# Residual additions over four tiles, and the squares of two norms summed with one column of ones

## The chip, the cores and the metric

One core of a Trainium2 chip runs the whole program. The metric is the time of one execution in microseconds of device time; the kernel before was run three times. TensorE (PE in the profile) multiplies, VectorE (DVE) and ScalarE (ACT) work element by element, GpSimd (POOL) and SyncE (SP) mostly issue transfers here.

## What is computed

Two transformer-like blocks one behind the other on 256 tokens of width 2048. The place of the change is the residual path with its norms: the end of the first block, and the start of the second.

```python
def rms_norm(v, g):
    vf = v.astype(F32)
    y = vf * lax.rsqrt(jnp.mean(vf * vf, axis=-1, keepdims=True) + RMS_EPS)
    return (y * g.astype(F32)).astype(v.dtype)

# first block
y, yc = hybrid_mixer(h, hc, rows, not last, w_in[i], conv_p, ssd_p, fourier_out[i], rwkv_p, w_o[i])
x = x + g1 * rms_norm(y, norm_g[i, 1])
h = rms_norm(x, norm_g[i, 2]) * (1 + sc2) + sh2
x = x + g2 * rms_norm(sq_relu_mlp(h, mlp_up[i], mlp_down[i]), norm_g[i, 3])
# second block
h = rmsnorm(x, g_mix[l]) * (1.0 + sc1) + sh1
x = x + gt1 * hybrid_mixer_2(h, w_in[l], ...)
h = rmsnorm(x, g_ffn[l]) * (1.0 + sc2) + sh2
x = x + gt2 * conv_glu_ffn(h, w_ffn_gate[l], ...)
return rmsnorm(x, final_g)
```

## The kernel before

Everything is float32 and lies transposed: a tile is 128 of the 2048 features on the partitions by 256 tokens (`T`), and there are 16 tiles (`KT`). `xT` holds the residual, `hT` the normed input of the next products, `work` scratch, `ps` the eight PSUM banks. Weights stream in units of one megabyte (`ring`), and each is split into a rounded part (`round_unit`, L2662, ScalarE) and its remainder (`rest_unit`, L2667, VectorE), so that products of rounded halves give float32 accuracy (L2700 to L2704 and, for the first two units behind a norm, L2721 to L2725 in `twin_products`). The order of work on each engine is the order in which the code of the stages is written for it: for the part that matters, `Mix` (out-projection, norm of y, residual, norm of x), `Mlp`, `In2`, `Ffn2`. Engines wait for one another by counting semaphores.

A norm is an object of `Rms`. There are two sorts.
- The norms of y (`rms_y1` behind the out-projection, `rms_y2` behind the MLP) and two later ones of x (`rms_x3`, `rms_x4`) are *summed*: ScalarE squares each tile as it comes out of the products (`square_out`, L2556), VectorE adds the squares of all tiles but the last (`add_square`, L2565), and TensorE sums over the partitions with the squares as the stationary operand and one column of ones, once for each half of the tokens (L2582, and L2585 for the last tile). That leaves 128x2 numbers with the tokens on the partitions. ScalarE takes the root (L2605), VectorE the reciprocal (L2610), and TensorE spreads the two columns over all partitions (`spread_root`, L2594) into a PSUM bank, `rows`.
- The norms in front of the MLP and of the in-projection (`rms_x1`, `rms_x2`) are not: ScalarE squares pairs of tiles of `xT` into `hT` as the residual is added (L2602, `nadd` counts tiles added), TensorE sums them with a full 128x128 of ones as the stationary operand and each tile of squares as 256 moving columns (L2577), which leaves the sum on every partition at once. Root and reciprocal are then taken over 128x256 in `rtn` in SBUF.

`add_scaled` (L2624) adds a normed y to the residual: for each tile one multiplication by the spread root (L2628), and one tile later a multiply by the gain and add (L2632). `scale_split` (L2635) and `shift_round` (L2648) then scale, shift and split x for the products: L2640 and L2644 on VectorE, L2651 on ScalarE. In `Mix`, VectorE has one `rest_unit` between `add_scaled` and the norm of x. In `Mlp` the last steps are `rms_y2`, `add_scaled`, and `In2` begins with `rms_x2`.

Other lines named below: L409 turns modulation rows with two moving columns and 128x128 stationary, early in the kernel; L3561 multiplies a tile of `xT` by the final gain on ScalarE; L3687 multiplies groups of four tiles by the spread root at the very end; L2745 copies the first half of a unit's result out of PSUM.

Of the kernel before, what the change touches and what calls it, by code (L numbers as in the profile page):

```python
# [13 lines left out]
P = 128  # L14
D = 2048
# [160 lines left out]
def branch_kernel(nc, x_t, ctx_t, vecs, consts, smalls, smalls2, c_rows, mod_u, mod_r, ada_r, conv_u, ssd_u, rw_u, gate_u, bo_u, wo_u,  # L176
                  mlp_u, in2_u, out2_u, ffn_u, down2_u, out_t):
    ctx = ExitStack()
    with ctx:
# [2354 lines left out]
        class Rms:  # L2534


            def __init__(self, src, ready, summed=0, reset=1, last=None, turns=1):
# [11 lines left out]
                self.rows = rtn  # L2549
                if summed:  # L2550
                    self.spread = aux()
                    self.rows = ps[:, self.spread[0], 0:T]
# [18 lines left out]
            def tensor(self, pe):  # L2571
                acquire(pe, self.use)
                if not self.summed:
                    for kt in range(KT):
                        if kt % self.step == 0:
                            pe.wait_ge(nsq, self.first + kt // self.step + 1)
                        mm = pe.matmul(ps[:, self.use[0], 0:T], kc("ones"), self.squares[:, kt, :], start=kt == 0, stop=kt == KT - 1)  # L2577
                    mm.then_inc(bk.full[self.use[0]], 1)
                    return
                pe.wait_ge(sq_added, self.total)  # L2580
                for a in range(TT):
                    pe.matmul(ps[:, self.use[0], a:a + 1], sq_sum[:, a * P:(a + 1) * P], kc("ones", 0, 1), start=a == 0, stop=False)  # L2582
                pe.wait_ge(nsq, self.first + self.summed)
                for a in range(TT):
                    mm = pe.matmul(ps[:, self.use[0], a:a + 1], self.last[:, a * P:(a + 1) * P], kc("ones", 0, 1), start=False, stop=a == TT - 1)  # L2585
# [11 lines left out]
            def scalar(self, act):  # L2597
# [6 lines left out]
                to, n = (root[:, 0:TT], TT) if self.summed else (rtn, T)  # L2604
                emptied(self.use, act.activation(to, ps[:, self.use[0], 0:n], ACT.Sqrt, bias=eps(EPS_RMS), scale=1.0 / D))  # L2605

            def vector(self, dve):
                evacuated(dve, self.use)
                to = root[:, 0:TT] if self.summed else rtn
                dve.reciprocal(to, to).then_inc(nrs, 1)  # L2610
                if self.summed:
                    full(dve, self.spread)
                else:
                    dve.wait_ge(nrs, self.k)

            def read(self, eng):
                if self.summed:
                    eng.sem_inc(bk.free[self.spread[0]], 1)
# [5 lines left out]
        def add_scaled(dve, own, src, col, rms):  # L2624

            for kt in range(KT + 1):
                if kt < KT:
# [1270 lines left out]
```

## Time and profile before

| | us |
|---|---|
| median of 3 runs (lowest, highest) | 3307.74 (3307.04, 3309.56) |
| profiled execution, its own time | 3307.34 |
| its span | 3305.7 |
| PE busy | 3227.1 (98%) |
| DVE busy | 2204.6 (67%) |
| ACT busy | 1241.4 (38%) |

The span is the time from the first to the last instruction of the profiled execution. The busy times say how full each engine is, but not what sets the end; that is to be read from the chain of work that ended last and from the timeline around the two places where the changed lines run, about 1456 to 1475 us and 2198 to 2216 us. The granted clock is given as a share of 2.4 GHz: 1.00 is 2.4, 0.50 is 1.2.

### The profile page before, as it was taken

Reading aid. Unit: us, or ns where it says so; the run is one execution under the profiler, and the core shown is the slowest. Engines: PE = TensorE matmul, PEld = TensorE weight load, DVE = VectorE, ACT = ScalarE, POOL = GpSimd, SP = SyncE. Lnnn points to the kernel's source line nnn. Section 1 sums busy time; section 2 is a strip of 40 time slices with the busy share of each in tenths; the row PEclk is TensorE's granted clock in tenths of the full one; section 3 lists DMA queues with packets and bytes.
Section 4 is the critical chain, followed back from the end, with each engine's and each line's share of the span. In section 5 each row is a group of like instructions: output and inputs, shape, how many; then the busy total and the mean of one; then the engine's idle time right before and its main releaser. Section 6 shows DMA issues by size and latency. Waiting matters only on the chain.

```text
span 3305.7 us, 58756 instructions
## 1 busy us (share of the span) xinstructions
PE 3227.1 (98%) x23408; PEld 2700.4 (82%) x23408; DVE 2204.6 (67%) x3396; ACT 1241.4 (38%) x1686; POOL 196.2 (6%) x298
## 2 busy tenths in 40 slices
PE   7999999999999999989999999989999999999998
PEld 4764685478888999978888888878888888888887
DVE  2377656665655677667878777787666667667667
ACT  2202130144444421344344444444544443443444
POOL 0000000012122000000000000000000000000000
PEclk9999999999999999999999999999999999999999
DMA  9956727622222688637767777745445557656654
GB/s 408 364 204 229 277 86 258 241 84 89 89 92 98 234 353 349 228 140 258 276 244 271 256 256 259 255 169 180 161 153 178 191 190 261 210 190 241 225 179 156
DMA packets 101013, 709.02 MB, mean 214 GB/s; under 512 B 11200, under 2 KB 11328, under 8 KB 19520
## 3 DMA queue, kind: packets, MB, share of 16 engines
q1 hardware_dynamic: 73872, 525.89, 43.9%
q0 software_dynamic: 23184, 169.88, 13.9%
q10 hardware_dynamic: 3744, 10.23, 0.8%
q8 instruction: 155, 2.54, 0.3%
q14 instruction: 58, 0.48, 0.0%
HBM read 698.36 MB, written 7.60 MB: 214 GB/s over the span
## 4 chain that ended last, share of the span: by engine, by line
PE 92%; DVE 4%; DMA 2%; issue 1%; ACT 1%; DVEq 0%; SPq 0%; ACTq 0%; POOLq 0%
PE ps L2704 33%; PE ps L2703 17%; PE ps L632 11%; PE ps L2407 3%; PE ps L1099 3%; PE ps L399 2%; PE ps L2700 2%; PE ps L1819 2%; PE ps L1100 2%; PE ps L1101 2%; PE ps L1833 1%; PE ps L2389 1%; PE ps L2388 1%; PE ps L2390 1%; PE ps L1091 1%; PE ps L2701 1%
## 5 line engine op out<-in xcount | busy, mean ns | idle before, releaser
L2704 PE MATMUL ps<-hT_parts,rows_parts 128*128 128x512 f32 x3210 | 1130.6, 394 | 0.0
L2703 PE MATMUL ps<-hT_parts,ring_parts 128*128 128x256 f32 x3210 | 901.9, 281 | 1.7 <-DVE hT_parts L2676 1.6
L2667 DVE TENSOR_TENSOR ring_parts<-ring,rows_parts 128x2048 fp32r<-128x2048 f32 (+1 forms) x337 | 762.1, 2262 | 102.7 <-ACT rows_parts L2662 101.7
L2662 ACT ACTIVATE rows_parts<-ring 128x2048 fp32r<-128x2048 f32 (+1 forms) x337 | 639.4, 1897 | 406.2 <-DMA ring<-in_mlp_u 209.1
L2704 PEld LDWEIGHTS ps<-hT_parts,rows_parts 128*128 128x128 f32 x3210 | 604.2, 188 | 125.0
L2703 PEld LDWEIGHTS ps<-hT_parts,ring_parts 128*128 128x128 f32 x3210 | 607.9, 189 | 12.6 <-DVE hT_parts L2676 2.9
L2704 PE MATMUL ps<-work_parts,rows_parts 128*128 128x512 f32 x1616 | 570.1, 395 | 0.0
L2703 PE MATMUL ps<-work_parts,ring_parts 128*128 128x256 f32 x1616 | 454.2, 281 | 0.0
L632 PE MATMUL ps<-hT,ring 128*128 128x512 f32 (+1 forms) x1088 | 372.4, 505 | 0.0
L2704 PEld LDWEIGHTS ps<-work_parts,rows_parts 128*128 128x128 f32 x1616 | 304.2, 188 | 63.2
L632 PEld LDWEIGHTS ps<-hT,ring 128*128 128x128 f32 x1088 | 206.9, 190 | 163.4 <-issue 152.0
L2745 ACT ACTIVATE work<-ps 128x256 f32<-128x256 f32 (+1 forms) x220 | 84.3, 383 | 616.5 <-PE ps L2704 608.3
L2703 PEld LDWEIGHTS ps<-work_parts,ring_parts 128*128 128x128 f32 x1616 | 306.2, 189 | 5.1
L2750 DVE TENSOR_TENSOR work<-work,ps 128x256 f32<-128x256 f32 (+1 forms) x220 | 92.6, 421 | 258.0 <-ACT work L2745 245.7
L433 DVE CUSTOM_DVE_ANT_0 rows<-rows 128x2048 f32<-128x2048 f32 x64 | 146.5, 2288 | 33.4 <-DMA rows<-in_mod_r 33.4
L2515 DVE CUSTOM_DVE_ANT_0 work<-work,K 128x2048 f32<-128x2048 f32 x64 | 146.3, 2286 | 0.0
L2407 PE MATMUL ps<-work 128*128 128x256 f32 x576 | 125.6, 379 | 0.0
L2407 PEld LDWEIGHTS ps<-work 128*128 128x128 f32 x576 | 109.0, 190 | 14.3
L2135 DVE TENSOR_TENSOR work<-work,ps 128x64 f32<-128x64 f32 x288 | 42.8, 216 | 115.5 <-PE ps L1833 114.4
L433 DVE CUSTOM_DVE_ANT_0 rows<-rows,K 128x2048 f32<-128x2048 f32 x32 | 73.3, 2290 | 49.1 <-DMA rows<-in_ada_r 49.1
L2508 POOL DMA_DIRECT2D work<-in_ada_r x64 | 33.8, 528 | 1204.4 <-DVE g_acc L2515 1171.3
L2836 DVE TENSOR_TENSOR work<-work,ps 128x256 f32<-128x256 f32 (+1 forms) x112 | 46.9, 418 | 80.6 <-PE ps L2704 80.3
(495 smaller groups left out, 4532.5 us busy)
## 6 DMA issues: line engine op xcount, KB each, us to landing
ring<-in_mlp_u SPq DMA_DIRECT2D x128, 1024.0 KB, 5.0
ring<-in_ffn_u SPq DMA_DIRECT2D x88, 1024.0 KB, 4.8
rows<-in_mod_r POOLq DMA_DIRECT2D x64, 1024.0 KB, 5.2
ring<-in_gate_u SPq DMA_DIRECT2D x64, 1024.0 KB, 5.2
work<-in_ada_r POOLq DMA_DIRECT2D x64, 1024.0 KB, 5.2
ring<-in_in_u SPq DMA_DIRECT2D x36, 1024.0 KB, 4.8
rows<-in_ada_r POOLq DMA_DIRECT2D x32, 1024.0 KB, 9.0
ring<-in_down_u SPq DMA_DIRECT2D x32, 1024.0 KB, 4.9
```

What stands on the lines that cost most here:

```text
L399: mm = pe.matmul(ps[:, use[0], o % 2 * T:(o % 2 + 1) * T], wtile(u, 4 * o + k), hT[:, 4 * kq + k, 0:T], start=kq + k + o % 2 == 0, stop=kq ...
L433: dve.tensor_tensor_reduce(rows_buf[:, j, :], rows_buf[:, j, :], conditioning, 1.0, 0.0, ALU.mult, ALU.add, g_acc[:, j:j + 1]).then_inc(ro ...
L632: mm = pe.matmul(outs[o], wtile(u + o, kt), rhs(kt), start=kt == 0, stop=kt == KT - 1)
L1099: pe.matmul(out, high, kept_high(kt), start=kt == 0, stop=False)
L2407: mm = pe.matmul(ps[:, 3 + b, o * T:(o + 1) * T], bo_buf[:, at + kt, o * P:(o + 1) * P], src[:, kt, :], start=kt == 0, stop=kt == kts - 1)
L2515: dve.tensor_tensor_reduce(late_row, late_row, c2_row, 1.0, 0.0, ALU.mult, ALU.add, acc).then_inc(late_free, 1)
L2662: act.activation(unit_high(u)[:, 0:size], slot(u)[:, 0:size], ACT.Copy).then_inc(hi_done, 1)
L2667: dve.tensor_tensor(ring_parts[:, ring_slot(u), 0:size], slot(u)[:, 0:size], unit_high(u)[:, 0:size].bitcast(F32), ALU.subtract)\
L2703: pe.matmul(ps[:, b, low_half], low, top(kt), start=False, stop=False)
L2704: mm = pe.matmul(ps[:, b, :], high, both(kt), start=False, stop=kt == kts - 1)
L2745: act.activation(dst, ps[:, b:b + 1, half], ACT.Copy).then_inc(half_out, 1)
L2750: dve.tensor_tensor(dst, dst, ps[:, b:b + 1, half], ALU.add).then_inc(bk.free[b], 1)
```

## The change

`add_scaled` goes over four tiles at a time. The multiplication by the spread root is one instruction over 128x1024, with the row repeated, and the addition one over 128x1024 (for the last group two over 128x512). The gain is no longer part of the addition: ScalarE multiplies y by it beforehand with a scaled copy in place (`scale_tile`), counted in `merge_sum`. In the out-projection this follows each tile's square; behind the MLP two tiles are scaled ahead of the root and fourteen behind it.

The norms `rms_x1` and `rms_x2` sum their squares in the form of the summed norms: for each of the 16 tiles two products, squares stationary, one column of ones moving. Their root and reciprocal go over 128x2, and TensorE spreads the result into the bank of the norm of y before them (`bank`). The squaring on ScalarE stays as it is.

```diff
-                self.rows = rtn
-                if summed:
-                    self.spread = aux()
-                    self.rows = ps[:, self.spread[0], 0:T]
+                self.spread = bk.take(bank) if bank else aux()
+                self.rows = ps[:, self.spread[0], 0:T]
...
-                        mm = pe.matmul(ps[:, self.use[0], 0:T], kc("ones"), self.squares[:, kt, :], start=kt == 0, stop=kt == KT - 1)
-                    mm.then_inc(bk.full[self.use[0]], 1)
-                    return
+                        for a in range(TT):
+                            mm = pe.matmul(ps[:, self.use[0], a:a + 1], self.squares[:, kt, a * P:(a + 1) * P], kc("ones", 0, 1),
+                                           start=kt == 0 and a == 0, stop=kt == KT - 1 and a == TT - 1)
                 mm.then_inc(bk.full[self.use[0]], 1)
                 acquire(pe, self.spread)
                 pe.wait_ge(nrs, self.k)
...
-                to, n = (root[:, 0:TT], TT) if self.summed else (rtn, T)
-                emptied(self.use, act.activation(to, ps[:, self.use[0], 0:n], ACT.Sqrt, bias=eps(EPS_RMS), scale=1.0 / D))
+                emptied(self.use, act.activation(root[:, 0:TT], ps[:, self.use[0], 0:TT], ACT.Sqrt, bias=eps(EPS_RMS), scale=1.0 / D))
...
-                to = root[:, 0:TT] if self.summed else rtn
-                dve.reciprocal(to, to).then_inc(nrs, 1)
-                if self.summed:
-                    full(dve, self.spread)
-                else:
-                    dve.wait_ge(nrs, self.k)
+                dve.reciprocal(root[:, 0:TT], root[:, 0:TT]).then_inc(nrs, 1)
+                full(dve, self.spread)
...
-        def add_scaled(dve, own, src, col, rms):
-
-            for kt in range(KT + 1):
-                if kt < KT:
-                    own.step(dve.tensor_tensor(src[:, kt, :], src[:, kt, :], rms.rows, ALU.mult))
-                if kt:
-                    own.settle(1 if kt < KT else 0)
-                    t = kt - 1
-                    dve.scalar_tensor_tensor(xT[:, t, :], src[:, t, :], col[:, t:t + 1], xT[:, t, :], ALU.mult, ALU.add).then_inc(nadd, 1)
+        def scale_tile(act, y, gain):
+
+            act.activation(y, y, ACT.Copy, scale=gain).then_inc(merge_sum, 1)
+
+        def add_scaled(dve, own, src, rms, scaled):
+
+            for g in range(KT // 4 + 1):
+                if g < KT // 4:
+                    group = src[:, 4 * g:4 * g + 4, :]
+                    dve.wait_ge(merge_sum, scaled + 4 * (g + 1))
+                    own.step(dve.tensor_tensor(group, group, bc(rms.rows, 4), ALU.mult))
+                if g:
+                    own.settle(1 if g < KT // 4 else 0)
+                    size = 4 if g < KT // 4 else 2
+                    for t in range(4 * (g - 1), 4 * g, size):
+                        dve.tensor_tensor(xT[:, t:t + size, :], xT[:, t:t + size, :], src[:, t:t + size, :], ALU.add).then_inc(nadd, size)
             rms.read(dve)
...
-        rms_x1 = Rms(xT[:, :, :], lambda e, n: e.wait_ge(nadd, 2 * n + 2))
+        rms_x1 = Rms(xT[:, :, :], lambda e, n: e.wait_ge(nadd, 2 * n + 2), bank=rms_y1.spread[0])
...
-                        rms_y1.square_out(act, yT1[:, bass.ds(it * 4 + j, 1), :], sq1[:, bass.ds(it * 4 + j, 1), :])
+                        t = bass.ds(it * 4 + j, 1)
+                        rms_y1.square_out(act, yT1[:, t, :], sq1[:, t, :])
+                        scale_tile(act, yT1[:, t, :], gn1[:, t])
...
-                add_scaled(dve, own, yT1, gn1, rms_y1)
+                add_scaled(dve, own, yT1, rms_y1, 2 * PAIRS2)
...
+                for t in range(2):
+                    scale_tile(act, yT2[:, t, :], gn3[:, t:t + 1])
                 rms_y2.scalar(act)
+                for t in range(2, KT):
+                    scale_tile(act, yT2[:, t, :], gn3[:, t:t + 1])
...
-                add_scaled(dve, own, yT2, gn3, rms_y2)
+                add_scaled(dve, own, yT2, rms_y2, 2 * PAIRS2 + KT)
...
-        rms_x2 = Rms(xT[:, :, :], lambda e, n: e.wait_ge(nadd, KT + 2 * n + 2))
+        rms_x2 = Rms(xT[:, :, :], lambda e, n: e.wait_ge(nadd, KT + 2 * n + 2), bank=rms_y2.spread[0])
```

## Rows read from the trace of the kernel before

**Rows 1.** The page, chain of work that ended last, by engine

```profile
PE 92%; DVE 4%; DMA 2%; issue 1%; ACT 1%; DVEq 0%; SPq 0%; ACTq 0%; POOLq 0%
```

**Rows 2.** Timeline, VectorE: start us, us, engine, line, operation, count [idle before <-releaser]

```profile
1456.68 0.75 DVE L2628 TENSOR_TENSOR work<-work,ps 128x256 f32<-128x256 f32 x2 [0.87 <-PE ps L2594]
1457.35 0.48 DVE L2632 SCALAR_TENSOR_TENSOR xT<-work,coef,xT 128x256 f32<-128x256 f32 x1
...
1467.51 0.89 DVE L2632 SCALAR_TENSOR_TENSOR xT<-work,coef,xT 128x256 f32<-128x256 f32 x2
...
1472.58 1.28 DVE L2640 SCALAR_TENSOR_TENSOR hT<-xT,coef,work 128x256 f32<-128x256 f32 x3
```

**Rows 3.** Timeline, the same stretch, ScalarE

```profile
1458.59 0.63 ACT L2602 ACTIVATE hT<-xT 128x512 f32<-128x512 f32 x1 [1.18 <-DVE xT L2632]
...
1470.29 0.47 ACT L2605 ACTIVATE work<-ps,K 128x256 f32<-128x256 f32 x1 [1.22 <-PE ps L2577]
...
1487.11 0.38 ACT L2745 ACTIVATE work<-ps 128x256 f32<-128x256 f32 x1 [2.41 <-PE ps L2725]
```

**Rows 4.** Timeline, the same stretch, TensorE; one product is several records

```profile
1459.37 8.31 PE L2577 MATMUL ps<-hT,K 128*128 128x256 f32 x24 [2.72 <-ACT hT L2602]
1468.00 2.25 PE L2577 MATMUL ps<-hT,K 128*128 128x256 f32 x8 [0.32 <-ACT hT L2602]
1474.40 0.47 PE L2721 MATMUL ps<-hT_parts,rows_parts 128*128 128x512 f32 x1 [4.15 <-DVE hT_parts L2644]
```

**Rows 5.** Stretches: busy time (records) of PE, PEld, DVE, ACT, POOL; PEclk, DMA, GB/s

```profile
1453.40:1458.20 4.80, 1.56 (x11) 1.23 (x10) 2.10 (x7) 2.83 (x4) 0.00 (x0) 1.00 0.65 218
1458.30:1465.00 6.70, 5.63 (x13) 4.56 (x14) 6.70 (x19) 3.11 (x5) 0.00 (x0) 0.50 0.00 0
1465.10:1475.20 10.10, 5.62 (x25) 3.84 (x23) 9.88 (x19) 4.18 (x8) 3.51 (x1) 1.00 0.00 0
1475.40:1478.70 3.30, 3.30 (x12) 2.82 (x12) 3.30 (x10) 2.09 (x5) 0.00 (x0) 0.50 0.02 5
...
2550.60:2557.30 6.70, 5.86 (x18) 5.06 (x19) 6.70 (x18) 4.58 (x11) 1.13 (x3) 0.50 0.47 157
```

**Rows 6.** Timeline and one line's instructions (ns least/median/most), TensorE: L409, L2577

```profile
22.55 1.84 PE L409 MATMUL ps<-K,work 128*128 128x2 f32 x8 [0.81 <-ACT work L416]
...
31.53 1.05 PE L409 MATMUL ps<-K,work 128*128 128x2 f32 x8 [0.72 <-ACT work L416]
...
L409 PE MATMUL ps<-K,work x8: 345/353/353, 22.6 to 24.0; 128*128 128x2 f32 x8
...
L2577 PE MATMUL ps<-hT,K x64: 378/385/766, 1459.4 to 2211.8; 128*128 128x256 f32 x64
```

**Rows 7.** Timeline around the norm in front of the second block's FFN

```profile
2547.67 0.61 PE L2585 MATMUL ps<-K,work 128*128 128x1 f32 x4 [1.56 <-ACT work L2556]
2548.92 0.68 PE L2594 MATMUL ps<-K,root 128*128 128x128 f32 x4 [0.64 <-DVE root L2610]
2549.64 1.26 DVE L2640 SCALAR_TENSOR_TENSOR hT<-xT,coef,ps 128x256 f32<-128x256 f32 x3 [0.87 <-PE ps L2594]
2551.44 0.77 PE L2721 MATMUL ps<-hT_parts,rows_parts 128*128 128x512 f32 x1 [1.84 <-DVE hT_parts L2644]
...
2565.11 0.38 ACT L2745 ACTIVATE work<-ps 128x256 f32<-128x256 f32 x1 [3.42 <-PE ps L2725]
```

**Rows 8.** Timeline at the end of the kernel, ScalarE and VectorE

```profile
3295.21 0.49 ACT L3561 ACTIVATE xT<-xT,V 128x256 f32<-128x256 f32 x1
...
3297.40 4.08 DVE L3687 TENSOR_TENSOR xT<-xT,ps 128x1024 f32<-128x1024 f32 x4 [0.94 <-PE ps L2594]
```

**Rows 9.** Timeline between MLP and in-projection, ScalarE and VectorE

```profile
2196.64 0.26 ACT L2605 ACTIVATE root<-ps,K 128x2 f32<-128x2 f32 x1 [1.09 <-PE ps L2585]
2198.58 0.76 DVE L2628 TENSOR_TENSOR work<-work,ps 128x256 f32<-128x256 f32 x2 [0.87 <-PE ps L2594]
...
2214.55 1.28 DVE L2640 SCALAR_TENSOR_TENSOR hT<-xT,coef,work 128x256 f32<-128x256 f32 x3
```

More of the change, by code:

```diff
@@ L2534, in branch_kernel, with __init__ @@
         class Rms:
-            def __init__(self, src, ready, summed=0, reset=1, last=None, turns=1):
+            def __init__(self, src, ready, summed=0, reset=1, last=None, turns=1, bank=None):
                 self.src, self.ready, self.summed = src, ready, summed
@@ L2572, in tensor @@
                 acquire(pe, self.use)
-                if not self.summed:
+                if self.summed:
+                    pe.wait_ge(sq_added, self.total)
+                    for a in range(TT):
+                        pe.matmul(ps[:, self.use[0], a:a + 1], sq_sum[:, a * P:(a + 1) * P], kc("ones", 0, 1), start=a == 0, stop=False)
+                    pe.wait_ge(nsq, self.first + self.summed)
+                    for a in range(TT):
+                        mm = pe.matmul(ps[:, self.use[0], a:a + 1], self.last[:, a * P:(a + 1) * P], kc("ones", 0, 1), start=False, stop=a == TT - 1)
+                else:
                     for kt in range(KT):
@@ L2576, in tensor @@
                             pe.wait_ge(nsq, self.first + kt // self.step + 1)
-                        mm = pe.matmul(ps[:, self.use[0], 0:T], kc("ones"), self.squares[:, kt, :], start=kt == 0, stop=kt == KT - 1)
-                    mm.then_inc(bk.full[self.use[0]], 1)
-                    return
[L2580 to L2585, printed above, removed]
+                        for a in range(TT):
+                            mm = pe.matmul(ps[:, self.use[0], a:a + 1], self.squares[:, kt, a * P:(a + 1) * P], kc("ones", 0, 1),
+                                           start=kt == 0 and a == 0, stop=kt == KT - 1 and a == TT - 1)
                 mm.then_inc(bk.full[self.use[0]], 1)
@@ L2603, in scalar @@
                 full(act, self.use)
-                to, n = (root[:, 0:TT], TT) if self.summed else (rtn, T)
-                emptied(self.use, act.activation(to, ps[:, self.use[0], 0:n], ACT.Sqrt, bias=eps(EPS_RMS), scale=1.0 / D))
+                emptied(self.use, act.activation(root[:, 0:TT], ps[:, self.use[0], 0:TT], ACT.Sqrt, bias=eps(EPS_RMS), scale=1.0 / D))
             def vector(self, dve):
                 evacuated(dve, self.use)
-                to = root[:, 0:TT] if self.summed else rtn
-                dve.reciprocal(to, to).then_inc(nrs, 1)
-                if self.summed:
-                    full(dve, self.spread)
-                else:
-                    dve.wait_ge(nrs, self.k)
+                dve.reciprocal(root[:, 0:TT], root[:, 0:TT]).then_inc(nrs, 1)
+                full(dve, self.spread)
             def read(self, eng):
-                if self.summed:
-                    eng.sem_inc(bk.free[self.spread[0]], 1)
+                eng.sem_inc(bk.free[self.spread[0]], 1)
         def load_root(act):
             act.activation(root[:, TT:TT + 1], eps(ONE), ACT.Sqrt)
-        def add_scaled(dve, own, src, col, rms):
-            for kt in range(KT + 1):
-                if kt < KT:
-                    own.step(dve.tensor_tensor(src[:, kt, :], src[:, kt, :], rms.rows, ALU.mult))
-                if kt:
-                    own.settle(1 if kt < KT else 0)
-                    t = kt - 1
-                    dve.scalar_tensor_tensor(xT[:, t, :], src[:, t, :], col[:, t:t + 1], xT[:, t, :], ALU.mult, ALU.add).then_inc(nadd, 1)
+        def scale_tile(act, y, gain):
[11 more added lines that the diff above has]
+                        dve.tensor_tensor(xT[:, t:t + size, :], xT[:, t:t + size, :], src[:, t:t + size, :], ALU.add).then_inc(nadd, size)
             rms.read(dve)
```

## The prediction

> **What bounds the kernel now.** I read the chain that ended last first: TensorE holds 92% of it, DVE 4% [rows 1]. So what the change touches off TensorE's path is worth nothing, and the question is where TensorE sits idle or works on the norms. The timeline shows two such places, alike: A, between out-projection and MLP (1453 to 1475 us), and B, between MLP and in-projection (2194 to 2216 us). Nothing else is ready for TensorE there, so every us of a junction is a us of the kernel.
>
> In A the reader is to see four pieces in a row. DVE multiplies and adds the residual tile by tile from 1456.68 to 1468.40 [rows 2]. ScalarE squares each pair of tiles behind it, and TensorE sums them with a full square of ones, from 1459.37 to 1470.25 [rows 3, 4]. Then root and a 256-wide reciprocal: 2.29 us from the start of the root at 1470.29 to the first scaling at 1472.58 [rows 2, 3]. Then the first products start at 1474.40, and the first pair of units is out at 1487.07, just ahead of the copy at 1487.11 [rows 3, 4]. B repeats this: 15.97 us from the first multiplication to the first scaling, against 15.90 in A [rows 2, 9].
>
> The clock matters as much. TensorE is granted 1.00 in the stretch to 1458.2, in which it does little, 0.50 (1.2 GHz) from 1458.3 to 1465.0, 1.00 again after five us of 256-wide products, and 0.50 once more from 1475.4 to 1478.7, after it had stood still from 1470.25 to 1474.40 [rows 4, 5].
>
> **The change, part by part.** I work in A with t = 0 at 1456.68 and take over to B.
>
> *Residual over four tiles.* Sixteen multiplications and sixteen multiply-adds, 0.73 us a tile (11.72 us in all), become four multiplications of 128x1024 with the PSUM row repeated, and five additions. The same multiplication stands at the kernel's end: 3.5 such groups in 4.08 us, 1.17 us each [rows 8]. The additions are not in the trace; with the same elements I take 1.17 per 1024 too (a bound from above is the 0.36 per 256 that the present pair averages, 1.46 per 1024). Sum 8 x 1.17 = 9.4 us instead of 11.7. But the first additions come later: multiply, multiply, add ends at t+3.5, where now the first pair is ready at about t+1.9 (square starts at 1458.59 [rows 3]). The first square ends at t+3.5+0.05+0.63 = t+4.2, that is 1460.88, and TensorE starts 1.5 us later than now.
>
> *Gain moved to ScalarE.* Sixteen scaled copies per norm. The like of it is the copy by the final gain, 0.49 us [rows 8]. In the out-projection loop it delays only weight rounding, which runs units ahead, and at the end of the loop it fits before the root, which waits for TensorE: nothing. At B two copies come ahead of the root, which idles there for 1.09 us [rows 9]: nothing. Fourteen stand behind it and ahead of the first square: from 2196.90, at some 0.40 each (0.49 less the usual overlap of a tenth), to 2202.5, where the first square could start at 2198.58+3.55 = 2202.1. So +0.4 us at B; at 0.32 each nothing, at 0.49 about +1.6.
>
> *Sum of squares with one column of ones.* This is the part that decides. Now each tile is one product of 256 columns, two records (32 per junction), with the ones loaded each time. After, each tile is two products of one column, four records, each with its own load of 128 columns of squares: 64 records per junction, and the load is the work. Its price depends on the clock. The turning of the modulation rows is the same form (128x128 stationary, two columns): eight records in 1.84 us at 22.55 with 353 ns each, and eight in 1.05 us at 31.53 [rows 6]. That is (1.84-0.353)/7 = 0.212 us from record to record in the one and, against the four in 0.61 us of the later norm [rows 7], (1.05-0.61)/4 = 0.11 in the other. I read the first as 1.2 GHz: the 256-wide sums show the same doubling, 378 to 766 ns [rows 6]. The grant printed for those early us is no help, as no change of it had been recorded by then.
>
> Which of the two holds? The clock must fall as now: from the end of the spread, just ahead of 1456.68, TensorE has nothing until 1460.88, longer than today. What brought it back in A was a run of 256-wide products. The new run has a load every 0.2 us and one column behind it; no row of this trace shows the clock rising in such a run, and the short runs of this form at the later norm were followed by a fall (0.50 from 2550.6 to 2557.3 [rows 5, 7]). I take it to stay at 1.2 GHz. Then squares arrive faster than TensorE takes them (a pair of tiles costs 1.7 us), and the sum ends at 1460.88 + 63 x 0.212 + 0.353 = 1474.59 instead of 1470.25: **+4.3 us**. The bound from the other side is 0.11 per record, below.
>
> The Trainium skill, page "TensorE: Matmul & The Clock Gate", section "LDWEIGHTS (loading the stationary operand)", prices a load by its columns alone, 128 of them at about 107 ns, with no word of the clock. By that figure 64 records are 6.8 us and TensorE keeps up with the squares, which is the second rival. The rows at 1.2 GHz speak against it.
>
> *Root, reciprocal, spread.* Now 2.33 us from the end of the sum to the first scaling. The later norm already does the new form at full clock: its sum ends at 2548.28, the scaling starts at 2549.64, 1.36 us [rows 7]. At 1.2 GHz its spread (four records, 0.68) would take some 1.0, so 1.69: **-0.64 us**. The first scaling in A moves from 1472.58 to 1476.28, +3.7; in B +3.6+0.4 = +4.0. Scaling out of PSUM instead of SBUF is 1.26 against 1.28 for three: nothing [rows 2, 7].
>
> *The products behind it.* They follow the scaling at the same distance. In A they took 12.67 us with 3.3 us of them at 1.2 GHz, at the later norm 13.63 (2551.44 to 2565.07) with 5.9 [rows 3, 4, 5, 7]: 0.38 us lost per us at the low clock. With little but loads before them they should start low in both junctions and stay so for between 3 and 6 us: 0 to +1.0 in A, 0 to +1.2 in B; I take **+0.5 and +0.6**.
>
> *Bank and waits.* The second norm of each pair spreads into the first one's bank, which DVE has let go before; the wait of the grouped multiplications for the scaled copies is met (at B, tile 7 is needed at 2199.8 and done at about 2199.4). Nothing else is queued behind them.
>
> **Sum.** A +3.7+0.5 = +4.2, B +4.0+0.6 = +4.6, together +8.8 us. All later work is TensorE's own chain and shifts with it. The profiled execution took 3307.34 us (span 3305.7 and 1.6 around it), so 3316.1; the median of the runs, 3307.74, is 0.4 above it: **3316.5 us**. Its own range: 3315.0 with no longer low clock and no wait for the copies, 3318.8 with all upper bounds, and down to 3313.5 if the clock returns late in one of the sums.
>
> **Rivals.**
> *First, the clock comes back during the sum* (ends within 0.2%). For: TensorE is never idle between the 64 records, as it never was in the run that raised the clock. Against: those were 256 columns wide. Back 5.6 us after the start, as in A now: 26 records by then, 38 more at 0.11 and 0.25 for the last, end at 1470.9, +0.6; tail at full clock -0.97; the products may start at full clock, which at 0.38 per us would give back some 1.2 and, as DVE then sets their pace, I take for at most 0.7. Per junction -0.4 to -1.1, B 0.4 worse, in all about -1: 3306.7 (3305.5 to 3308). It decides from the point where TensorE needs less than about 11 us for the sum.
> *Second, the low clock doesn't slow the loads, or never comes* (same or just faster). The third group is added by t+8.2 = 1464.9 and the rest by 1466.1, so the fifth pair is squared by 1465.5 and the eighth by about 1467.1; four pairs of 0.9 behind 1465.5 end at 1469.2, -1.0; tail -0.97; products 0 to -0.7. Twice -2.0 to -2.7: 3303 (3302 to 3304). This is also what the grouped residual is worth by itself. Against: the 353 ns rows.
> *Third, more of the same*: low clock, full 6 us of it after each junction, copies at 0.49 and additions at 1.46 us per 1024: 3319 to 3321.
>
> **How the numbers follow.** Forecast 0.60, first rival 0.24, second 0.09, third 0.07. What a measurement of this kernel can tell from no change is about 0.2%, 6.6 us: slower means above 3314.4, faster below 3301.1. Slower gets 0.54 of the forecast's 0.60 and the third's 0.07, 0.61; faster 0.04 out of the second; the rest, 0.35, is within. The range of 8 in 10 reaches into the rivals: 3303.0 to 3319.5, the forecast's own being 3313.5 to 3319.
>
> **What would show it.** In the new profile: the grouped residual in about 9.4 us; 64 one-column records per junction, 0.21 us apart at a grant of 0.50; the sum's end near 1474.6 and 18 us after the first multiplication in B; 1.4 to 1.7 us from there to the first scaling; the first products low from their start. Wrong if the grant is 1.00 during the sum, or if the records stand 0.11 apart at 0.50; or if the squares, not TensorE, end last.

## The result and the profile after

The changed kernel takes 3316.39 us (median of 22 runs, 3313.26 to 3320.87), the kernel before in the same comparison 3309.51 us (22 runs, 3305.02 to 3313.51): a ratio of 1.0021, 95% interval 1.0016 to 1.0027, or 6.9 us more (5.3 to 8.9). The profiled executions differ by 7.9 us of span, 3313.6 against 3305.7. The whole interval lies above 1, so the change makes the kernel slower; the size is right at the 0.2% that was named ahead as what can be told from no change, and the interval reaches to both sides of it.

Junction A after, TensorE (start us, us, engine, line, operation, count, [idle before <-releaser]):

```profile
1454.23 1.20 PE L2593 MATMUL ps<-K,root 128*128 128x128 f32 x4 [0.64 <-DVE root L2607]
1459.76 13.79 PE L2583 MATMUL ps<-K,hT 128*128 128x1 f32 x64 [4.33 <-ACT hT L2601]
1474.18 1.19 PE L2593 MATMUL ps<-K,root 128*128 128x128 f32 x4 [0.64 <-DVE root L2607]
```

The same stretch on VectorE:

```profile
1455.46 2.35 DVE L2627 TENSOR_TENSOR work<-work,ps 128x1024 f32<-128x1024 f32 x2 [1.38 <-PE ps L2593]
...
1462.26 2.42 DVE L2632 TENSOR_TENSOR xT<-xT,work 128x1024 f32<-128x1024 f32 x3
...
1475.41 1.26 DVE L2640 SCALAR_TENSOR_TENSOR hT<-xT,coef,ps 128x256 f32<-128x256 f32 x3 [1.38 <-PE ps L2593]
```

And on ScalarE:

```profile
1458.98 1.15 ACT L2601 ACTIVATE hT<-xT 128x512 f32<-128x512 f32 x2 [3.30 <-DVE xT L2632]
...
1463.52 2.19 ACT L2601 ACTIVATE hT<-xT 128x512 f32<-128x512 f32 x4 [1.12 <-DVE xT L2632]
1473.58 0.26 ACT L2603 ACTIVATE root<-ps,K 128x2 f32<-128x2 f32 x1 [7.87 <-PE ps L2583]
...
1490.05 0.38 ACT L2745 ACTIVATE work<-ps 128x256 f32<-128x256 f32 x1 [2.59 <-PE ps L2725]
```

These answer to [rows 2 to 4]. VectorE is done with the residual at 1464.68, 9.22 us after its first multiplication (11.72 before), and ScalarE has the last square at 1465.71. But ScalarE's root then waits 7.87 us more for TensorE, where it waited 1.22 before: the 64 records run without a pause from 1459.76 to 1473.55. What VectorE saves does not reach the end of the junction, because TensorE has become its bound.

The stretches after (from:to, us, busy time and records of PE, PEld, DVE, ACT, POOL, granted clock, DMA share, GB/s), against [rows 5]:

```profile
1459.80:1473.50 13.70, 13.70 (x64) 13.65 (x64) 7.09 (x7) 3.67 (x7) 3.51 (x1) 0.50 0.01 2
1473.60:1480.90 7.30, 4.87 (x16) 4.15 (x17) 5.65 (x15) 3.82 (x9) 0.00 (x0) 0.50 0.00 0
1481.10:1490.00 8.90, 8.90 (x53) 7.84 (x52) 7.01 (x18) 4.15 (x9) 0.53 (x1) 1.00 0.11 16
```

The grant is 0.50 through the whole sum and on into the products; before, it had come back to 1.00 in the middle of the sum. B is alike: 0.50 in every stretch from 2201.3 to 2228.3.

To compare kernels whose junctions start at different times I count from the first residual multiplication, t, to the first pair of units copied out by ScalarE (for A here 1490.05 - 1455.46 = 34.59 us, before 1487.11 - 1456.68 = 30.43). In B it is 34.79 against 30.29. Together: 69.38 against 60.72, **+8.66 us**. This "junction time" is used for every run below.

It leaves out the spread of the norm of y just ahead of t. In the profiled execution of the change that spread took 1.20 us in A, all of it at 0.50, and 1.04 in B, most of it at 0.50, against 0.68 and 0.68 before. Counted from the start of VectorE's last instruction on products ahead of each junction (1452.05 and 2197.84; before 1453.79 and 2194.68) the change takes 9.55 us more and not 8.66. That the change causes the slower spread isn't shown: in the run with 128 columns below, with the same code up to there, the spread takes 0.68 us in A and 1.20 in B.

### The profile page after: what moved, and what is told of

Its sections match the earlier page's. It is cut to its first block, busy times and chain, and to the rows that moved or that the text cites. A ratio compares the mean times of both kernels' runs of the same rounds, so it can differ in the third digit from the quotient of the medians.

```text
span 3313.6 us, 58911 instructions
## 1 busy us (share of the span) xinstructions
PE 3235.6 (98%) x23480; PEld 2712.2 (82%) x23480; DVE 2196.2 (66%) x3350; ACT 1252.7 (38%) x1718; POOL 196.2 (6%) x298
## 4 chain that ended last, share of the span: by engine, by line
PE 91%; DVE 4%; DMA 2%; issue 1%; ACT 1%; DVEq 0%; SPq 0%; POOL 0%; POOLq 0%; ACTq 0%
PE ps L2704 33%; PE ps L2703 17%; PE ps L632 11%; PE ps L2407 3%; PE ps L1099 3%; PE ps L399 2%; PE ps L2700 2%; PE ps L1819 2%; PE ps L1100 2%; PE ps L1101 2%; PE ps L1833 1%; PE ps L1091 1%; PE ps L2701 1%; PE ps L2388 1%; PE ps L2389 1%
## 5 line engine op out<-in xcount | busy, mean ns | idle before, releaser
L2703 PE MATMUL ps<-hT_parts,ring_parts 128*128 128x256 f32 x3210 | 900.9, 281 | 2.0 <-DVE hT_parts L2676 2.0
L2750 DVE TENSOR_TENSOR work<-work,ps 128x256 f32<-128x256 f32 (+1 forms) x220 | 92.6, 421 | 257.4 <-ACT work L2745 244.9
L2390 PE MATMUL ps<-hT_parts,ring_parts 128*128 128x256 f32 x352 | 99.4, 283 | 0.0
```

The costliest lines, as they stand in the source:

```text
L2390: mm = pe.matmul(out, low, h_high[:, kt, :], start=False, stop=kt == KT - 1)
L2703: pe.matmul(ps[:, b, low_half], low, top(kt), start=False, stop=False)
L2750: dve.tensor_tensor(dst, dst, ps[:, b:b + 1, half], ALU.add).then_inc(bk.free[b], 1)
```

## The experiments

All were timed beside the kernel before, whose medians were 3307.36, 3308.63, 3308.30 and 3307.88 us in the four sets. The theory: the one-column sum costs 64 loads at the low clock, starts late because of the grouped residual, and TensorE sets the end. The rivals: the residual or the root and spread carry the difference, or the price of a record is not one of the clock.

**The residual alone.** The changed kernel with the class Rms of before; the gain copies and the four-tile groups stay.

> Only the grouped residual and the scaled copies; the norms of x as before (ones stationary, 256 columns moving, two records of 0.27 us a tile at 2.4 GHz, 0.43 at 1.2). Theory (TensorE at the low clock ends the sum last): squares come 1.5 us later at first, so TensorE starts at t+4.3 instead of t+2.7 after the first multiplication, works some 5.6 us at 1.2 GHz and ends near t+15.0 instead of t+13.6; the whole kernel is 2 to 3 us slower than before, although DVE is done 2.3 us earlier in each junction. Rival (the residual sets the end): what DVE saves arrives, 2.3 us per junction, 4 to 5 us faster.

Ratio 0.9997 (0.9988 to 1.0006); junction times 30.21 and 29.87, 0.64 us less in all. TensorE in A:

```profile
1459.47 9.29 PE L2577 MATMUL ps<-hT,K 128*128 128x256 f32 x32 [4.33 <-ACT hT L2602]
```

and its two stretches:

```profile
1459.50:1463.70 4.20, 4.20 (x10) 3.40 (x11) 4.20 (x5) 1.97 (x4) 0.00 (x0) 0.50 0.00 0
1463.90:1468.70 4.80, 4.80 (x23) 3.94 (x21) 2.71 (x2) 1.52 (x3) 3.52 (x1) 1.00 0.01 2
```

Neither expectation was right, neither 2 to 3 us slower nor 4 to 5 faster. The sum starts 1.6 us later than before (t+4.29 for t+2.69) and ends where it did, 13.58 us after t against 13.57. Before, the sum was stretched over the pairs of squares as they came (32 records in 10.9 us [rows 4]); now the squares are ahead of it, and it works at 0.42 us a record until the clock is back (10 in 4.20 us) and 0.21 behind that (23 in 4.80). TensorE's own work sets the end here too, so the 2.5 us that VectorE saves don't arrive.

**The norm alone.** The kernel before with the new Rms (one column of ones, narrow root, spread).

> Only the sum with one column of ones and the spread root; the residual tile by tile as before. Theory: TensorE starts at t+2.7 and needs 64 records of 0.212 us at 1.2 GHz: end near t+16.4, +2.8; the shorter root and reciprocal give back 0.5; products behind it up to +0.4: +2.5 per junction, 5 us slower than before, and 1.5 us per junction better than the whole change, whose late first square it does not have. Rival (the late first square is what costs, not the form of the sum): no slower than before.

Ratio 1.0015 (1.0006 to 1.0024), +5.0 us as expected; junction times 33.44 and 33.23, +5.95.

```profile
1462.28 13.78 PE L2583 MATMUL ps<-K,hT 128*128 128x1 f32 x64 [2.72 <-ACT hT L2601]
```

The same 13.8 us, started 2.69 us after t. So the new norm makes the loss. The parts don't add: -0.64 and +5.95 make 5.3, both together 8.66. The grouped residual takes 0.64 us off the junctions under the wide sum and adds 2.71 under the narrow one. Under the narrow sum its first square, 1.6 us later, is paid in full: the first scaling moves from 18.34 and 18.40 us after t to 19.95 and 20.02, 3.2 us in the two junctions, of which the products behind give back 0.5. Under the wide sum the later start is absorbed.

**The clock raised ahead of the sum.** The changed kernel with eight idle products in front of the sum.

```
 else:
+    for n in range(8):
+        pe.matmul(ps[:, self.use[0], T:2 * T], kc("ones"), K[:, 0:T], start=True, stop=True)
     for kt in range(KT):
```

> The whole change, and ahead of the first square eight more products of 256 columns of constants into an unused half of the sum's bank, to fill the 4.3 us in which TensorE stands still. Theory (the clock is the price of a record): the grant is 1.00 at the start of the sum and the records stand 0.11 us apart as long as it lasts. If it lasts through the sum, the squares set the end, the sum is over near t+11.3 and the first scaling comes at t+12.7 instead of t+20.0: 12 to 14 us below the whole change, 5 to 7 below the kernel before. If the loads let it fall on the way, something between. Rival (a load of squares costs 0.21 us at any clock): the sum takes 13.8 us as before and the time is that of the whole change.

Ratio 1.0013 (1.0004 to 1.0022); junction times 31.95 and 33.22, 4.21 us less than in the changed kernel: the case in between that was expected if the loads let the clock fall on the way. The sum in A, the sum in B, and the stretches in A:

```profile
1462.83 3.70 PE L2585 MATMUL ps<-K,hT 128*128 128x1 f32 x32
1466.85 6.21 PE L2585 MATMUL ps<-K,hT 128*128 128x1 f32 x32 [0.32 <-ACT hT L2603]
...
2206.23 11.65 PE L2585 MATMUL ps<-K,hT 128*128 128x1 f32 x64
```

```profile
1461.00:1462.80 1.80, 1.80 (x10) 1.59 (x9) 1.80 (x3) 1.15 (x2) 0.00 (x0) 1.00 0.00 0
1462.90:1467.60 4.70, 4.38 (x40) 4.29 (x38) 4.70 (x6) 2.58 (x5) 0.20 (x1) 1.00 0.02 5
1467.80:1473.00 5.20, 5.20 (x25) 5.18 (x25) 1.74 (x1) 0.56 (x2) 3.11 (x1) 0.50 0.00 0
```

Two things are shown. At a grant of 1.00 the same records stand (3.70 - 0.167)/31 = 0.114 us apart, not 0.213: the price of a record goes with the clock. And the one-column records not only don't bring the clock back, it falls again under them. In A a wait of 0.32 us lies ahead of the fall at 1467.7; in B there is none, the 64 records run without a pause from 2206.23, and the grant falls all the same, at 2208.4.

That it is the load of 128 columns that costs the 0.213 us, and not a fixed price of any record, is argued and not tested: no run varied the load. The trace of before has a row that speaks against a fixed price, with loads of a quarter of the size, at a grant of 0.50: 64 records in 1.93 us.

```profile
714.65 1.93 PE L1833 MATMUL ps<-work 64*64 64x32 f32 x64
```

**Squares and ones rounded to fp32r, two equal columns.** One record for a half tile instead of two, 32 per junction. The squares lose low bits by it.

> The whole change, but the squares and the ones of the two norms of x are written rounded (fp32r), so that each product is one pass, 32 records per junction instead of 64, two equal columns of ones moving. The squares lose low bits by that. Theory: at 1.2 GHz a one-pass load costs at most half of 0.212 x 2 a product; the sum keeps up with the squares and ends at t+10.6, the first scaling comes at t+12.5 instead of t+15.9 before: 6 to 7 us faster than before. If each record costs 0.21 whatever its passes, TensorE needs 6.8 us and ends near t+11.4: 4 to 5 us faster. Rival (the number of records is not what costs): no better than the whole change.

Ratio 0.9991 (0.9982 to 1.0000); junction times 28.97 and 28.58, -3.17.

```profile
1460.96 1.84 PE L2584 MATMUL ps<-K_parts,hT_parts 128*128 128x2 f32 x8 [4.33 <-ACT hT_parts L2602]
```

Eight records in 1.84 us, 0.21 apart, as the fp32 ones: rounding by itself makes no record cheaper, and half the number of records is worth all of the loss and more. The gain is short of the 4 to 5 us expected for this price: the sum ends at t+12.30 and not near t+11.4. The grant stays 0.50 throughout the sum.

**A smaller first group.** The changed kernel with residual groups of 2, 4, 4, 4 and 2 tiles.

> The changed kernel with its residual in groups of 2, 4, 4, 4 and 2 tiles in place of 4, 4, 4 and 4. Nothing is left out. Theory (the sum of one-column products is bound by TensorE, 64 records at 0.215 us, so the time at which it starts is paid in full at its end): the first two tiles are ready 1.1 us sooner, TensorE starts 3.1 us after the first residual multiplication instead of 4.30, waits some 0.4 us for the next pairs, and the first scaling comes 18.9 instead of 19.95 us after the first multiplication in both junctions; 2 us less than the changed kernel, a ratio of about 1.0015 to the kernel before. Rival (the end of the sum is set by the last squares, as in the kernel before): the first scaling stays at 19.95 us and the ratio at 1.0021.

```profile
1457.84 1.84 PE L2583 MATMUL ps<-K,hT 128*128 128x1 f32 x8 [3.27 <-ACT hT L2601]
1460.01 12.11 PE L2583 MATMUL ps<-K,hT 128*128 128x1 f32 x56 [0.34 <-ACT hT L2601]
```

Ratio 1.0029 (1.0018 to 1.0039), so the expected 1.0015 is missed. In A the sum does start 1.07 us earlier and the first scaling comes 0.57 earlier, 19.38 us after t. But the first copy comes at 34.59 us after t, exactly as in the changed kernel: the clock is at 0.50 until 1480.7, now for 6.7 us behind the first scaling and not 5.6, and the products lose what the sum had gained. In B the fourteen gain copies on ScalarE hold up the earlier first square until 2204.37, 3.81 us after t, the clock is at 0.50 for 7.5 us behind the first scaling (6.3 in the changed kernel), and the junction takes 35.73, 0.94 more than in the changed kernel.

**256 rounded squares through ones.** The sum of before on top of the grouped residual, with fp32r squares and ones: 16 records.

```
-mm = pe.matmul(ps[:, self.use[0], 0:T], kc("ones"), self.squares[:, kt, :], ...)
+mm = pe.matmul(ps[:, self.use[0], 0:T], ones_r, self.squares[:, kt, :], ...)
```

> The residual of the changed kernel (four tiles at a time) with the sum, root and reciprocal of the kernel before (ones as the operand that is loaded, 256 squares flowing, full-width root and reciprocal), but with squares and ones rounded to fp32r, so that a tile takes one record and not two. Theory: a record costs what it loads or streams at the granted clock, at most 0.21 us here, so 16 records take 3.4 us and never set the end; the sum ends 0.4 to 0.5 us behind the last square, which the run with the grouped residual alone has 10.2 us after the first multiplication; with the old tail of 2.33 us the first scaling comes at 13.0 us after the first multiplication in both junctions (15.90 before, 19.95 in the changed kernel, 14.2 in the one-column form with rounded squares). The products behind may start at the low clock and give back up to 0.5 us in each: 4.8 to 5.8 us less than before in all, a ratio of 0.9983 to 0.9986. Rival (what TensorE or VectorE saves here is given back behind the junction, as with the grouped residual alone): the first scaling comes early, but the ratio is 0.9995 or above.

Ratio 0.9992 (0.9983 to 1.0001); first scaling 13.43 and 13.49 us after t (13.0 expected), junction times 27.72 and 27.93, 5.07 less than before.

```profile
1462.67 2.36 PE L2578 MATMUL ps<-hT_parts,K_parts 128*128 128x256 f32 x8 [0.95 <-ACT hT_parts L2603]
1469.18 0.76 PE L2729 MATMUL ps<-hT_parts,rows_parts 128*128 128x512 f32 x1 [4.15 <-DVE hT_parts L2652]
```

TensorE now waits 0.95 us for squares: they end last. The junctions did what the theory says; the runs showed about half of it, -2.6 us, with -5.1 inside the interval (-5.6 to +0.3). The profiled execution shows no place between the junctions where the rest is lost (from the first copy behind A to VectorE's last instruction on products ahead of B 707.55 us, 707.57 before). Behind B's first copy it takes 0.95 us more than before, where the fourteen traces differ by 1.5.

**The same with eight idle products ahead of it.**

> The kernel of the rounded 256-column sum with eight idle products of TensorE more (fp32, 256 columns, results not read) between the spread of the norm before and the sum. They take about 5 us from just behind the spread, so they end some 0.6 us after the first squares are there, and at most 8 of the 16 records wait for that. Theory (the low clock comes with TensorE's idle time in front of the sum): the granted clock is back at 1.00 during the sum and still is when the twin products start; the sum ends where it does without them, and the products behind give 0.4 us back in each junction: a ratio 0.0002 below that of the same kernel without them. Rival (the sum's own few short records let the clock fall again, as the one-column records did): the clock is 0.50 again at the first twin product and the time is the same within 0.5 us.

Ratio 0.9983 (0.9974 to 0.9992), the fastest run here. The expected mechanism isn't what did it: in A the grant was 1.00 during the sum and 0.50 again from 1464.5, before the first product, and in B 0.50 again from 2205.2.

```profile
1457.80:1464.40 6.60, 4.38 (x22) 3.00 (x20) 6.60 (x7) 4.24 (x8) 1.10 (x1) 1.00 0.00 1
1464.60:1474.60 10.00, 5.85 (x19) 4.81 (x19) 9.86 (x21) 5.25 (x11) 2.22 (x1) 0.50 0.01 2
```

The junction times, 28.79 and 27.80, are 0.94 us more in all than without the idle products. The two ratios' intervals overlap, so a gain from the idle products is not shown.

**More columns of ones through each record.** The changed kernel with 64 and with 128 equal columns in place of one (for 128):

```
-mm = pe.matmul(ps[:, self.use[0], a:a + 1], self.squares[:, kt, a * P:(a + 1) * P], kc("ones", 0, 1),
+mm = pe.matmul(ps[:, self.use[0], 128 * a:128 * a + 128], self.squares[:, kt, a * P:(a + 1) * P], kc("ones", 0, 128),
```

with the root reading one column of each half.

> The changed kernel, with 64 equal columns of ones flowing through each record of the two sums in place of one (each half's result stands 64 times; the root reads one of them). Nothing is left out; number of records and of loads is the same. The question is what sets a record's 0.215 us at the low clock and what keeps the clock there. Theory A (the load of 128 columns sets the price, and the clock does not come back because hardly anything flows): 64 columns flow beside the load and cost nothing by themselves (0.11 us by half of the 256-column record's 0.43 us at the low clock and its proportion), and the clock may come back as it does under the 256-column records, about 4 to 7 us after the start of the sum; the records behind that take 0.115 us, the sum 9 to 11 us in place of 13.8, the first scaling 15.5 to 17.5 us after the first multiplication in place of 19.95: 5 to 9 us less than the changed kernel, ratio 0.9995 to 1.0007. Theory B (the loads by themselves keep the clock low, whatever flows): 13.8 us again, first scaling at 19.95 us, ratio 1.0021.

64 columns: ratio 1.0023 (1.0014 to 1.0032), junction times 34.81 and 34.70.

```profile
1461.09 13.89 PE L2583 MATMUL ps<-K,hT 128*128 128x64 f32 x64 [4.33 <-ACT hT L2601]
```

A stream of 64 columns adds nothing to a record, (13.89 - 0.421)/63 = 0.214 us a record as with one, and the grant stays at 0.50: this far it is theory B.

> As the run with 64 columns, with 128 columns of ones through each record. By proportion to the 256-column record (0.43 us at the low clock, 0.21 at full) a record's stream takes 0.21 us at the low clock, as long as the load now takes. Theory A (the clock follows what flows): the same price per record, the clock comes back 4 to 7 us into the sum, sum of 9 to 11 us, first scaling at 15.5 to 17.5 us after the first multiplication, ratio 0.9995 to 1.0007; if 64 columns did not bring the clock back, these do. Theory B (the loads keep it low): first scaling at 19.95 us or later, ratio 1.0021 or more.

128 columns: ratio 0.9988 (0.9979 to 0.9997), junction times 28.73 and 29.47, 2.52 less than before and 11.2 less than the changed kernel.

```profile
1463.34 9.11 PE L2583 MATMUL ps<-K,hT 128*128 128x128 f32 x64 [4.33 <-ACT hT L2601]
```

```profile
1463.40:1466.90 3.50, 3.50 (x17) 3.50 (x18) 3.50 (x4) 1.47 (x3) 0.00 (x0) 0.50 0.00 0
1467.10:1472.40 5.30, 5.30 (x48) 5.16 (x47) 3.38 (x3) 2.19 (x4) 3.52 (x1) 1.00 0.02 5
1472.50:1487.70 15.20, 12.76 (x68) 10.11 (x69) 12.86 (x33) 8.20 (x17) 0.53 (x1) 1.00 0.00 0
```

Same number of records and of loads as in the changed kernel, 128 times as many columns, of which one is read, and the clock comes back 3.6 us into the sum. The first 17 records stand 0.21 us apart, the rest 0.11, and the first scaling comes at t+14.77 and t+14.81. In A the products run at full clock as well; in B the grant is 0.50 once more from 2217.9 to 2221.3, as it was before the change. It was even better than theory A had it (15.5 to 17.5). The return isn't the luck of one execution: in the three runs with 128 fp32 columns the grant comes back in all six sums, 7.6 to 8.5 us after t, and in the eight sums of the four runs that have 1 or 64 columns and no idle products in none.

> The changed kernel with squares and ones rounded to fp32r (one record for each half tile, 32 in place of 64) and 128 equal columns of ones through each record. With two columns in place of 128 the first scaling came 14.2 us after the first multiplication at the low clock throughout, where the last square is done at 10.25 and the tail takes 1.7 to 1.9. Theory A (the clock follows what flows): the clock comes back behind the first third of the records, the backlog of about 10 records at the last square is then worked off in 1.1 us, and the first scaling comes at 13.2 us; products behind at full clock: 6 us less than before, ratio 0.9982 to 0.9986. Theory B (the loads keep it low): the first scaling at 14.2 us as with two columns, ratio 0.9991.

One record per half tile with 128 columns: ratio 0.9992 (0.9983 to 1.0001), first scaling at t+14.29 and t+14.36, junction times 29.18 and 29.21. Here the grant stayed at 0.50 through both sums, as theory B had it, in single rounded records with 0.24 to 0.30 us of waiting between the groups. Which of the two differences from the run with 64 fp32 records keeps it there, the waiting or the single rounded record, isn't shown; that loads by themselves keep the clock low is not what the runs with 128 fp32 columns say.

**128 columns with the residual tile by tile, and 128 columns once more.**

> The new norm with 128 columns of ones through each record, and the residual of the kernel before (one tile at a time), so that the sum starts 2.7 us after the first residual multiplication and not 4.3, and its pairs of squares come 1.45 us apart, the last at 12.4 us. Nothing is left out. Theory A (with a stream of 128 columns the clock comes back although TensorE waits between the pairs, as it does in the kernel before): a pair's eight records take 0.94 us at full clock, so the sum ends 0.9 to 1.0 us behind the last square, at 13.3 us, and the first scaling comes at 14.7 us after the first multiplication, the same as with the grouped residual (14.8); ratio about 0.9988. Then the grouped residual adds nothing to this form. Theory B (the pauses between the pairs keep the clock low): eight records take 1.72 us, longer than a pair's 1.45, the sum ends at 16.5 us, the first scaling comes at 18.3 us as in the run with the norm alone; ratio about 1.0015.

Ratio 0.9999 (0.9990 to 1.0008); first scaling at t+14.96 and t+15.03, junction times 28.99 and 29.63, -2.10.

```profile
1459.83 8.39 PE L2583 MATMUL ps<-K,hT 128*128 128x128 f32 x48 [2.72 <-ACT hT L2601]
1468.46 2.28 PE L2583 MATMUL ps<-K,hT 128*128 128x128 f32 x16 [0.24 <-ACT hT L2601]
```

The clock was back at 1465.7, 5.9 us into the sum, in spite of the earlier start, and the first scaling is near theory A's 14.7. The ratio is neither theory's: A's 0.9988 lies just outside the interval, B's 1.0015 far outside. And the pauses on which theory B rested didn't occur: at 0.50 the records were slower than the squares, and the only waits, 0.24 us in A and 0.29 in B, came after the clock was back. So this run says nothing on pauses. The grouped residual is worth 0.4 to 0.6 us of junction time under this sum, as under the wide one.

> The changed kernel with 128 columns of ones through each record, once more, on the same chip and beside the same runs of before as the kernel with the residual tile by tile. If the first comparison (0.9988) holds: first scaling at 14.8 us after the first multiplication in both junctions, ratio 0.998 to 0.9995. If that comparison was chance: the ratio is at 1.000 or above although the scaling comes at the same time.

Ratio 0.9991 (0.9982 to 1.0000), junction times 28.82 and 29.25, -2.65. The first comparison repeats, -4.0 and -3.0 us by the runs and -2.5 and -2.65 by the junctions: some 10 us less than the change as made. The gain over before is small; it was on the same side twice, and the second interval just reaches 1.

All runs together; the last column is (ratio - 1) times the median of before in that set:

| kernel | sum's records, columns | first scaling after t, A, B | junction times less before's 60.72 | runs |
|---|---|---|---|---|
| before | 32, 256 | 15.90, 15.97 | 0 | 0 |
| change | 64, 1 | 19.95, 20.02 | +8.66 | +6.9 |
| residual_only | 32, 256 | 15.91, 15.37 | -0.64 | -1.0 |
| norm_only | 64, 1 | 18.34, 18.40 | +5.95 | +5.0 |
| warm8 | 64, 1 | 16.83, 18.53 | +4.45 | +4.3 |
| onepass_col | 32, 2 (fp32r) | 14.18, 14.25 | -3.17 | -3.0 |
| small_first | 64, 1 | 19.38, 20.30 | +9.60 | +9.6 |
| onepass_wide | 16, 256 (fp32r) | 13.43, 13.49 | -5.07 | -2.6 |
| warm_wide | 16, 256 (fp32r) | 13.33, 13.20 | -4.13 | -5.6 |
| cols64 | 64, 64 | 20.05, 20.13 | +8.79 | +7.6 |
| cols128 | 64, 128 | 14.77, 14.81 | -2.52 | -4.0 |
| cols128_again | 64, 128 | 14.80, 14.67 | -2.65 | -3.0 |
| onepass_128 | 32, 128 (fp32r) | 14.29, 14.36 | -2.33 | -2.6 |
| norm128 | 64, 128 | 14.96, 15.03 | -2.10 | -0.3 |

The intervals of the runs are some 3 us to either side. Within them the two junctions account for every kernel. The traces also show where single executions scatter: VectorE's last instruction on products ahead of A starts anywhere from 1451.0 to 1458.5 us, while from there on the fourteen traces differ by little outside the junctions: 706.3 to 708.5 us between A and B, 1076.3 to 1077.8 from B's first copy to the end.

That the clock in the traces is also that of the other executions can be read from the mean grant of each. It is 0.986 to 0.989 in all executions of the change, norm_only, small_first and cols64, whose grant stays at 0.50 through both sums and into the products, and 0.990 to 0.994 in all of before in the four sets and in all of the three runs with 128 fp32 columns.

## Why the prediction was right, and where its terms were off

The predicted 3316.5 stands beside 3316.39, closer than its steps deserve. The difference predicted was +8.8; the junctions show +8.66, the runs +6.9 (5.3 to 8.9). The base was the profiled execution of before plus 0.4, 3307.74, while before measured 3309.51 in the comparison: 1.8 us too low a base and 1.9 too large a difference cancel.

*Grouped residual.* 9.4 us predicted, 9.22 measured. Its additions, which the trace of before did not show, take 1.22 us each at a pitch of 1.13. TensorE starts 4.30 us after t, 4.20 predicted.

*The sum*, the step that decides, held: 64 records at 0.50, (13.79 - 0.352)/63 = 0.213 us apart (0.212 predicted), 13.79 us in all (13.71). It ends at t+18.09 against 17.91. The choice between 0.21 and 0.11 per record was the right one. That the price goes with the clock, the eight idle products showed; that the clock would stay low was taken from the want of a row to the contrary, and the runs with 1, 64 and 128 columns now bear it out.

*The page of the Trainium skill*, "TensorE: Matmul & The Clock Gate", section "LDWEIGHTS (loading the stationary operand)": it gives a load's time as its columns divided by 1.2, in ns, for 128 columns an estimate of 107 ns, and names neither clock nor type. The trace agrees at a grant of 1.00, with 0.114 us between records, and not at 0.50, with 0.213. The second rival, in which TensorE keeps up with the squares, is out.

*Root and spread.* -0.64 us predicted, -0.47 measured: the tail takes 1.86 us (1473.55 to 1475.41), since the scaling starts 1.23 us behind the spread's start at this clock. First scaling +4.05 us in A instead of +3.7.

*The copies of the gain at B.* +0.4 predicted, nothing measured, and that by luck: they end at 2205.65 and the first square starts at 2205.63, as late after t (3.52 us) as in A. There was no margin left, and the copies were in time only because the spread ahead of t took 1.04 us and not 0.68, which put t itself later. In the three runs with the copies whose spread in B took 0.68 us (warm8, small_first, onepass_128) the first square starts 3.81, 3.81 and 3.82 us after t, 0.3 later. So the term was real, about 0.3 us, and hidden behind one that the prediction lacked, the next.

*A term that was missing.* The spread of the norm of y was taken to be as before. It took 0.52 and 0.36 us longer at the lower clock. The rise of 8.8 us leaves that out, as the junction time does.

*The products behind.* +0.5 and +0.6 predicted, +0.11 and +0.45 measured. The rate of 0.38 us lost per us of low clock is too simple. In A the time from the first scaling to the first copy was 13.96 us with no low clock at all (128 columns), 14.29 with 4.8 us of it from the first scaling on (256 rounded columns), 14.64 with 5.6 (the change), 15.10 with 7.1 (norm alone), 15.46 with 7.4 (warm_wide). Of a low clock from the start the first us cost little and the later ones more. But before, 3.4 us at 0.50 that began 2.7 us behind the first scaling went with 14.53, more than the 4.8 us of the rounded columns did: it also matters where the low clock falls. That VectorE's scaling sets the pace at first, so that a slow TensorE costs nothing there, would fit; no run tested it.

*The first rival* (the clock comes back in the sum, -1 us in all) was not what happened here, but it is what 128 columns make of the same kernel, with -2.5. I had weighed it by the absence of pauses. That was not enough: 64 one-column records without a pause stayed at 0.50. The bound I gave, 11 us for the sum, isn't contradicted: 9.1 us with 128 columns wins, 13.8 loses, and nothing was measured in between with this form.

*Wrong in the working*: twice 2.0 to 2.7 us, of which the second rival says "This is also what the grouped residual is worth by itself." By itself it is worth 0.64 us of junction time. I let the squares set the end there and did not cost the wide sum's own records at the low clock, 0.42 us each.

## What to carry to other kernels

When a reduction on TensorE is made narrow, count its loads and not its columns, at the clock that holds in that stretch, and look at what the narrow stream does to the clock behind it: 64 one-column records at 0.50 took 13.8 us where the 32 wide ones of before took 10.9, pauses included. Before giving up such a form, let more equal columns flow beside the loads; here 128 columns cost nothing by themselves and turned +7 us into -3 or -4, while 64 changed nothing. And a part that is worth nothing by itself can cost something together with another (here 2.7 us of junction time), if it delays an engine that the other has made the bound.

## What the runs showed of the hardware that I had not expected

- A record with a load of 128 fp32 columns costs 0.213 us at a grant of 0.50 whether 1 or 64 columns flow (0.21 with 128), and 0.114 with one column at 1.00. At 1.00 with 128 columns it is 0.11 too (48 records in 5.30 us). With fp32r operands and 2 or 128 columns it is 0.21 to 0.22 at 0.50.
- TensorE at work without any pause is no assurance of the clock: it was at 0.50 through 13.8 us of records back to back, with 1 and with 64 columns, and fell from 1.00 to 0.50 in the middle of such a run, in B of warm8 without any pause, when idle products had raised it. With 128 columns in the same 64 records the grant went to 1.00 after 3.6 us; with 128 columns in 32 single rounded records and short pauses it did not.
- An earlier sum doesn't end the low clock earlier. With the smaller first group in A the first scaling came 0.57 us sooner after t, and the stretch at 0.50 ended 26.1 us after t against 25.5 in the changed kernel.
